# A reordered opening of the projection stage, key transposes without a staged copy, and an earlier load of the first remaining weight block

## What is computed

```python
h = rmsnorm(x, norm_pre);  p = in_proj(h, w_in)
# conv:  y = B * conv3(C * h_conv) * silu(z_conv), depthwise, causal, 256 channels
# nsa:   o = g0 * o_cmp + g1 * o_slc + g2 * o_win, g = sigmoid(gate), times silu(z)
x = x + rmsnorm(concat(nsa, gla, conv) @ w_out, norm_post)
```

## Time and profile before

| what | value |
|---|---|
| median of three executions | 1030.3 us |
| the profiled execution, its own time | 1031.92 us |
| its span | 1030.2 us |
| VectorE, ScalarE, GpSimd busy | 58%, 40%, 20% of the span |
| mean granted TensorE clock | 0.955 of full |
| most used DMA queue | 18.9% of 16 engines |

### The profile page before, as it was taken

The page is one execution under the profiler, slowest core; times in us unless marked ns, Lnnn a source line. Parts: engine busy times, 40 slices in busy tenths (PEclk is TensorE's granted clock), DMA queues, the critical chain, the costliest instruction groups (busy, mean ns, idle before and its releaser), DMA issues. The chain is left out here.

```text
span 1030.2 us, 16718 instructions
## 1 busy us (share of the span) xinstructions
PE 937.7 (91%) x5935; PEld 811.0 (79%) x5935; DVE 601.8 (58%) x1437; ACT 412.5 (40%) x918; POOL 201.7 (20%) x180
## 2 busy tenths in 40 slices
PE   2999999999969998999899978999788999999997
PEld 2999999999968987777789867777545676777765
DVE  3632010176434666778744567788648877787663
ACT  4533221111032545666534445666444434444322
POOL 3009599999320000000000050000000000000000
PEclk9999999999979999999999988999878999999999
DMA  6216634435051110000011012400334446453321
GB/s 208 93 53 198 245 103 142 162 112 165 1 180 43 52 42 28 9 1 1 1 43 50 23 46 68 138 1 1 140 112 115 117 135 187 135 150 103 117 88 32
DMA packets 106820, 93.73 MB, mean 91 GB/s; under 512 B 21245, under 2 KB 99954, under 8 KB 104626
## 3 DMA queue, kind: packets, MB, share of 16 engines
q1 hardware_dynamic: 84946, 58.65, 18.9%
q10 hardware_dynamic: 19488, 17.25, 5.5%
q0 software_dynamic: 2304, 16.78, 4.6%
HBM read 78.16 MB, written 18.61 MB: 94 GB/s over the span
## 5 line engine op out<-in xcount | busy, mean ns | idle before, releaser
L588 PE MATMUL ps<-w_hi,h_hi 128*128 128x264 f32 (+5 forms) x432 | 124.1, 287 | 0.5 <-DVE h_lo L457 0.5
L588 PE MATMUL ps<-w_hi,h_lo 128*128 128x264 f32 (+5 forms) x432 | 123.0, 285 | 0.0
L588 PE MATMUL ps<-w_lo,h_hi 128*128 128x264 f32 (+5 forms) x432 | 123.0, 285 | 0.0
L1276 DVE TENSOR_TENSOR pt_lo<-ps,pt_hi 128x512 fp32r<-128x512 f32 x132 | 90.9, 688 | 52.5 <-ACT pt_hi L1192 51.9
L1192 ACT ACTIVATE pt_hi<-ps 128x512 fp32r<-128x512 f32 x132 | 78.6, 597 | 83.5 <-PE ps L1099 82.7
L465 DVE TENSOR_TENSOR w_lo<-w_raw,w_hi 128x1024 fp32r<-128x1024 f32 (+2 forms) x12 | 29.1, 2426 | 122.4 <-ACT w_hi L366 122.4
L1272 DVE TENSOR_REDUCE least<-ps 128x1 f32<-128x640 f32 (+7 forms) x128 | 90.0, 703 | 14.0 <-PE ps L1088 12.7
L313 POOL TENSOR_TENSOR chunk<-chunk 128x1024 f32<-128x1024 f32 (+2 forms) x46 | 82.0, 1783 | 3.6
L588 PEld LDWEIGHTS ps<-w_hi,h_hi 128*128 128x128 f32 (+1 forms) x432 | 79.7, 185 | 1.3 <-issue 1.2
L588 PEld LDWEIGHTS ps<-w_lo,h_hi 128*128 128x128 f32 (+1 forms) x432 | 79.7, 184 | 0.0
L588 PEld LDWEIGHTS ps<-w_hi,h_lo 128*128 128x128 f32 (+1 forms) x432 | 79.4, 184 | 0.0
(11 more groups left out here) (382 smaller groups left out, 2285.5 us busy)
## 6 DMA issues: line engine op xcount, KB each, us to landing
kv_pages<-in_cache_slc_kv SPq DMA_DIRECT2D x256, 64.0 KB, 1.9
shared<-in_x_prompt SPq DMA_DIRECT2D x8, 512.0 KB, 3.6
w_raw<-in_w_in SPq DMA_DIRECT2D x8, 512.0 KB, 3.9
wr_raw<-in_w_in SPq DMA_DIRECT2D x8, 512.0 KB, 4.0
kv_window<-in_cache_win_kv SPq DMA_DIRECT2D x4, 1024.0 KB, 5.3
wo_raw<-in_w_out SPq DMA_DIRECT2D x8, 512.0 KB, 8.4
out<-in_cache_win_kv SPq DMA_DIRECT2D x1, 4032.0 KB
x_row<-in_x_prompt ACTq DMA_DIRECT2D x7, 512.0 KB, 5.1
```

What stands on the lines that cost most here:

```text
L588: mm = nc.tensor.matmul(out, lhs, rhs, start=(k == 0 and i == 0), stop=(k == KD - 1 and i == 2))
L1276: nc.vector.tensor_tensor(pt_lo[:, t % PTS, :], ps[:, turn_bank(t), :], pt_hi[:, t % PTS, :].bitcast(F32), ALU.subtract).then_inc(s_ptl, 1)
```

## The change

- VectorE starts with `normed(0)`; the page numbers come behind all tiles; the low halves of blocks 0 and 1 are VectorE's, after the scaled halves of tiles 0 and 1; `normed(t + 1)` stands between the two loops of `halves(t)`.
- The convolution's blocks are in the order c, h, z, b; a `b` take waits for the `z` take of the same columns.
- Rest block 0 is loaded in `project`, at the turn of block 8, into a place that the first stage does not use then (upper part of `w_raw`); three of its "w_split" steps stand ahead of the first "k_turn" and the fourth behind it.
- `k_st` and its copies are gone: TensorE transposes columns of `pk` with both key heads side by side, and ScalarE and VectorE read the 64 PSUM rows of their head.
- The gates' sigmoid is a tanh of ScalarE in `project` and one VectorE instruction (0.5 t + 0.5) at the start of `attend_prompt`.

```diff
...
+            at_w = -(-nc.sbuf_base // 32) * 32
+            w_next = nc.alloc_sbuf_tensor_at("wr_raw", [P, KD, P], F32, offset=at_w + 4 * KD * P)
...
-    CHAN = [("chbz"[m], h, c + h * P) for h in range(2) for m, c in enumerate((C_C, C_H, C_B, C_ZC))]
+    CHAN = [("chzb"[m], h, c + h * P) for h in range(2) for m, c in enumerate((C_C, C_H, C_ZC, C_B))]
...
+                    if b == NTB + 2:
+                        sp.dma_start(w_next[:, :, :], w_in[0, :, C_Z:C_Z + P].rearrange("(k p) c -> p k c", p=P)
+                                     ).then_inc(s_wr, 16)
...
-                for b in range(2):
-                    pool.wait_ge(s_whi, b + 1)
-                    nc.gpsimd.tensor_tensor(half(w_lo, b), raw(b), half(w_hi, b).bitcast(F32), ALU.subtract
-                                            ).then_inc(s_wlo, 1)
...
+                    if b == NTB:
+                        wait_taken(act, (NTB - 2, NT - 1))
+                        nc.scalar.activation(pk[:, 0:NT, K_GATE:NK], pk[:, 0:NT, K_GATE:NK], ACT.Tanh, scale=0.5)
...
                             ps[:, 6 + f, 0:4 * rows].rearrange("p (k c) -> p k c", k=4),
                             g_col[:, 4 * f:4 * f + 4].unsqueeze(2).to_broadcast([P, 4, rows]),
                             ALU.mult).then_inc(s_xg, 1)
+                    if t < 2:
+                        split(t)
+                    if t + 1 < T1:
+                        normed(t + 1)
                     for f in range(2):
                         dve.wait_ge(s_hi, 2 * t + f + 1)
                         nc.vector.tensor_tensor(
                                 src[:, n_p:tn].rearrange("p (b t) -> p b t", b=DB), ALU.mult)
                         ins.then_inc(s_td, 1)
                     elif what == "b":
+                        wait_taken(dve, (b - 1, c))
                         nc.vector.tensor_tensor(y_t[:, t0:t0 + tn], y_t[:, t0:t0 + tn], src, ALU.mult
                                                 ).then_inc(s_td, 1)
...
                         dve.wait_ge(s_tanh, n + 1)
                         did(nc.vector.scalar_tensor_tensor(tanh[:, n % 2, 0:tn], tanh[:, n % 2, 0:tn], 1.0, src,
                                                            ALU.add, ALU.mult))
-                        wait_taken(dve, (b - 1, c))
                         nc.vector.scalar_tensor_tensor(y_t[:, t0:t0 + tn], y_t[:, t0:t0 + tn], 0.5,
                                                        tanh[:, n % 2, 0:tn], ALU.mult, ALU.mult
                                                        ).then_inc(s_td, 1)
...
                 nc.vector.memset(eps[:, :], EPS).then_inc(s_ident, 1)
+                normed(0)
+                dve.wait_ge(s_g, 16)
+                for t in range(T1):
+                    halves(t)
                 dve.wait_ge(s_pg, 48)
                 dve.wait_ge(s_iota, 1)
                 did(nc.vector.tensor_scalar(page16[:, :], pages[:, :], float(NCH), None, ALU.mult))
                 nc.vector.tensor_tensor(rows16[:, :], chunk_no[:, :], page16[:, :].to_broadcast([P, NCH]),
                                         ALU.add).then_inc(s_idx, 1)
-                dve.wait_ge(s_g, 16)
-                normed(0)
-                normed(1)
-                for t in range(T1):
-                    halves(t)
-                    if t + 2 < T1:
-                        normed(t + 2)
                 split(2)
                 split(3)
                 dve.wait_ge(s_lo, 2 * T1)
...
-                    elif kind(b) == "z":
+                    elif kind(b) == "b":
                         v.wait()
                         wait_taken(dve, (b, 2))
                         nc.vector.memset(start[:, 0:1], 0.0).then_inc(s_conv, 1)
...
+                if kv == 0:
+                    for j in range(KD // 2 - 1):
+                        yield "w_split", 0, j
                 for b in range(4):
                     yield "k_turn", kv, b
-                    if b == 1 and kv == 0:
-                        for j in range(KD // 2):
-                            yield "w_split", 0, j
+                    if b == 0 and kv == 0:
+                        yield "w_split", 0, KD // 2 - 1
                     if b > 0 or kv > 0:
                         yield from fill(4)
...
-        w_raw = sb("wr_raw", [P, KD, P])
+        w_raw = w_next
         w_hi = sb("wr_hi", [P, KD, P], F32R)
+        sb("wr_raw_place", [P, KD, P])
         w_lo = sb("wr_lo", [P, KD, P], F32R)
...
-        k_st = prob[0][:, :, :].rearrange("p g n -> p (g n)")[:, 0:3 * NT * P].rearrange(
-            "p (n t a d) -> p n t a d", n=3, t=NT, a=2)
...
-        gate = sb("gate", [P, NT, 3 * NKV * NG])
+        gate = pk[:, 0:NT, K_GATE:NK]
...
-        s_wr, s_whi, s_wlo = sem("rest_w_loaded"), sem("rest_w_hi"), sem("rest_w_lo")
+        s_wr, s_whi, s_wlo = L.s_wr, sem("rest_w_hi"), sem("rest_w_lo")
...
-                load_w(0)
...
                     if what == "k_turn":
-                        if y == 0:
-                            pe.wait_ge(s_stg, x + 1)
                         if y >= 2:
...
                         for t in range(4):
-                            mm = nc.tensor.transpose(
-                                ps[:, 4 + 2 * (y % 2), t * P:(t + 1) * P],
-                                k_st[:, y // 2, 4 * (y % 2) + t, :, :].rearrange("p a d -> p (a d)"),
-                                ident[:, :])
+                            c = (K_SLC, K_WIN)[y // 2]
+                            mm = nc.tensor.transpose(ps[:, 4 + 2 * (y % 2), t * P:(t + 1) * P],
+                                                     pk[:, 4 * (y % 2) + t, c:c + NKV * HD], ident[:, :])
                         mm.then_inc(s_kt, 1)
...
                         for j in range(NT):
                             mm = nc.tensor.matmul(ps[:, 4, 2 * j:2 * j + 2],
-                                                  k_st[:, 2, j, :, :].rearrange("p a d -> p (a d)"), wk2[:, :],
+                                                  pk[:, j, K_CMP:K_CMP + NKV * HD], wk2[:, :],
                                                   start=True, stop=True)
...
-                nc.scalar.activation(gate[:, :, :], pk[:, 0:NT, K_GATE:NK], ACT.Sigmoid).then_inc(s_gate, 1)
-                nc.scalar.preload_act_table_set("exp_and_others")
...
                         b = y if what == "k_turn" else 4
                         act.wait_ge(s_kt, 6 * x + b + 1)
-                        dst = kT[:, b // 2, 512 * (b % 2):512 * (b % 2) + 512] if b < 4 else kcT[:, :]
-                        nc.scalar.activation(dst, ps[:, 4 + 2 * (b % 2), 0:512 if b < 4 else NB],
+                        dst = kT[0:HD, b // 2, 512 * (b % 2):512 * (b % 2) + 512] if b < 4 else kcT[0:HD, :]
+                        nc.scalar.activation(dst, ps[x * HD:(x + 1) * HD, 4 + 2 * (b % 2), 0:512 if b < 4 else NB],
...
+                nc.vector.tensor_scalar(gate, gate, 0.5, 0.5, ALU.mult, ALU.add).then_inc(s_gate, 1)
                 for what, x, y in steps:
                     if what == "k_stage":
-                        if x > 0:
-                            dve.wait_ge(s_pt, first_tile[PER_KV * x - 1])
-                        for a in range(2):
-                            for n, c in enumerate((K_SLC, K_WIN, K_CMP)):
-                                last = nc.vector.tensor_copy(k_st[:, n, :, a, :],
-                                                             pk[:, 0:NT, x * HD + c:x * HD + c + HD])
-                        last.then_inc(s_stg, 1)
                         if x == 0:
                             stage_query(0)
...
                     elif what in ("k_turn", "c_keys"):
                         b = y if what == "k_turn" else 4
                         dve.wait_ge(s_khi, 5 * x + b + 1)
-                        dst = kT[HD:P, b // 2, 512 * (b % 2):512 * (b % 2) + 512] if b < 4 else kcT[HD:P, :]
-                        nc.vector.tensor_tensor(dst, ps[HD:P, 4 + 2 * (b % 2), 0:512 if b < 4 else NB],
-                                                dst.bitcast(F32), ALU.subtract).then_inc(s_klo, 1)
+                        hi, lo = [kT[r, b // 2, 512 * (b % 2):512 * (b % 2) + 512] if b < 4 else kcT[r, :]
+                                  for r in (slice(0, HD), slice(HD, P))]
+                        nc.vector.tensor_tensor(lo, ps[x * HD:(x + 1) * HD, 4 + 2 * (b % 2), 0:512 if b < 4 else NB],
+                                                hi.bitcast(F32), ALU.subtract).then_inc(s_klo, 1)
```

More of the change, by code:

```diff
@@ L106, in hybrid_step @@
                 nc.sbuf_tensor("prob_win", [P, NG, WIN + P], F32) as prob_win:
-            project(nc, sem, ident, pq, pk, pn, kc, h_hi, h_lo, prob_win, s_cst, s_out, ps, va_dram, conv_dram,
+            at_w = -(-nc.sbuf_base // 32) * 32
+            w_next = nc.alloc_sbuf_tensor_at("wr_raw", [P, KD, P], F32, offset=at_w + 4 * KD * P)
+            project(nc, sem, ident, pq, pk, pn, kc, h_hi, h_lo, prob_win, s_cst, s_out, w_next, L.s_wr, ps, va_dram, conv_dram,
```

(8 more changed lines are left out.)

## The result

The changed kernel took 1013.93 us (median of five executions, 1013.81 to 1020.7); the kernel before, beside it, took 1028.99 us. The ratio is 0.9857, with a 95% interval of 0.9831 to 0.9882: 14.7 us (12 to 17) less, where 12.4 less and 1018 us had been forecast, in a range of 1010 to 1026. The profiled execution was the slowest of the five, 1020.7 us.

The account below looks back on a forecast made before the run. Time is won where TensorE, busy 937.7 of 1030.2 us, waits with nothing to do. Terms -7.7 + 2.8 - 6.0 - 1.5 + 0 gave -12.4 us, so 1018 us as a median, range 1010 to 1026.

Parts of the forecast that it names:

- The opening: Start of the first stage: block 0's product with tile 1 starts at 20.9 in place of 28.58, -7.7 us.
- The order: Block 10 in the first stage: z takes before the split delay its low half, stalling TensorE, +2.8 us.
- The multiply at 234.71 would meet the split: At block 10: beside GpSimd's 3.66 us multiply the split ends at 239.6, where TensorE needs it at 236.65.
- Rival 1: No stall at block 10, as GpSimd's phase has moved by 1.4 us and VectorE passes: 1013.6 us, chance 0.24.
- The border: Between first and second stage: keys turned at once, first rest product at 288.5 in place of 294.51, -6.0 us.
- The second key head: Before the second key head's transposes in the second stage: the wait for six key copies goes, -1.5 us.
- The clock: Granted clock behind waits: -1.5 us at the stage border, +1.5 behind block 10's stall, 0 together, bounds -4.5 and +3.5.
- The sum: All terms over the whole kernel: -7.7 + 2.8 - 6.0 - 1.5 + 0 = -12.4 us.
- Rival 3: First stage: x tiles arrive late and TensorE waits at seven tiles, so slower, 1037 us, chance 0.03.
- Rival 4: Rest block 0 is loaded during projections but split in the next stage; earlier splits give the same time; no chance given.

Follow-up runs that it names:

- the opening alone: Kernel before with only VectorE starting at tile 0, page numbers last and low halves of blocks 0 and 1 on VectorE: 1020.15 us, ratio 0.9914.
- border alone: Kernel before with only early load and splits of rest block 0, no key copies and gates by tanh: 1024.55 us, ratio 0.9944.
- the split ahead: Changed kernel with the split of block 10 ahead of the z takes on ScalarE and VectorE: 1007.45 us, and 1009.47 us once more.

## Why the prediction was right, step by step

- **The opening** (-7.7): measured -8.6 in the profile and 8.9 with the opening alone. Right. The 0.9 is gathered over VectorE's chain, which ends its last low halves of h at 19.84 and not at 20.7; the largest part, 0.5, are the low halves of h, 1.29 us for two where 1.47 was taken. The sum had left out that tile 2's transposes stand ahead of this product: from 19.3, with 1.94 us, they would have ended at 21.2. They took 1.09. The part that the text gave to page numbers against low halves was not priced separately; alone, the page numbers move the product by 2.1 us.
- **The order** (+2.8, bounds 0 and 5.6): the stall was 4.82 us, 4.8 to 4.9 in three profiles with this order and the gather in its place. Direction and mechanism were right, the size was not: the step that failed is "The multiply at 234.71 would meet the split". It met the third take, and the split then met an addition as well, 4.46 + 3.36 where the term had one meeting. The upper bound of 5.6 was this very case, with 4.47 and 3.92; it should have been the term. Taking the gain at the border off, this part costs more than it gives: undoing it gave 0.9778 against 0.9844.
- **Rival 1** (no stall, since GpSimd's phase has moved by 1.4 us): its time of 1014 was measured, but for another reason. The stall is there in the execution of 1013.67 us too, so that 1013.93 is nearer to this rival than to 1018 says nothing for it. Its premise was wrong twice: the page numbers end 0.3 us behind the tiles, and a first gather 13 us later left the phase at block 10 where it was.
- **The border** (-6.0): -6.5. Right. 0.9 us of it are the transposes at full clock, of which 0.5 was lost to the wait for the first low half. Without the early load and splits the border gives 1.8 us.
- **The second key head** (-1.5): its wait is gone. Right.
- **The clock** (0: -1.5 at the border, +1.5 behind the stall): it fell behind the stall as foreseen (5.7 us low), and cost 2.4 us in that piece and not 1.5. At the border it gave more than 1.5: 4.9 us low became 0.3 there, and 18.9 became 13.4 behind it, where the piece shrank by 4.2 with only 1.5 of it the second head's wait.
- **The sum**: from the first to the last piece but one the profiles differ by -14.2 us where -12.4 was forecast. The stall with its clock cost 6.6 and not 4.3; opening (-8.6), border with the stretch behind it (-10.7 in place of -9.0) and the last rest products (-1.5, no term) gave 4.1 more than forecast. So the total is close because misses of both signs cancel, which is luck in part. The last piece, where nothing was changed, then adds +3.0 in this pair of profiles. By the medians the miss is 2.3 to 2.7 us of 12.4.
- **Rival 3** (late tiles) did not show: no wait on the transposes beyond tile 2. **Rival 4**: the diff was what counted, as taken. Its "the same time" for earlier splits wasn't tried; the first rest product waited 0.50 us for a low half, so it needn't hold.

What stays open is the part of the clock in the sum of the parts. Opening and border alone give ratios of 0.9914 and 0.9944, together 0.986; the kernel with both and the old order has 0.9778, some 8 us less. The profiles put that into low clock: 92 us in the kernel before, 79 and 89 us with one part alone, 54 with both. Why fewer low stretches come when the two are joined isn't shown; a part may be chance, as the changed kernel alone went from 85 to 64 us between two profiles.

The best versions of the study that compute everything are the changed kernel with the split ahead (1007.45 and 1009.47 us, ratios 0.9772 and 0.9796) and the one with the old order (0.9778), which the measurements don't tell apart; the change itself has 0.9844 to 0.9857. The Trainium skill (SBUF — State Buffer, section "Who interferes with whom") says that a VectorE instruction with two SBUF inputs and a GpSimd instruction that reads SBUF shut each other out for a whole instruction; the 4.45 to 4.47 us beside 3.65, in all thirteen profiles that have the multiply, and 0.54 and 1.22 once GpSimd's sums are gone, agree with it.

## What to carry to other kernels

A reordering that puts more instructions ahead of a weight split has to be priced with more than one meeting with the neighbour engine: here a take met the multiply and the split behind it met the additions. Moving the split ahead of the takes cost nothing and won 5 to 9 us by the ratios. Two waits can cover each other, as the key copies and the load do here: with the copies alone gone the border gave 1.8 of 5.4 us (the early load alone wasn't tried). And a forecast finer than half a per cent needs to know how the granted clock varies between executions of one kernel: cutting two profiles at the same instructions shows which pieces differ, and how much low clock each has.

## What the runs showed of the hardware that I had not expected

- VectorE and GpSimd fall into step: in thirteen profiles GpSimd's multiply starts 0.64 or 0.65 us behind one VectorE instruction of the convolution and 0.39 or 0.40 us behind one of a z take. With the first gather 13 us later a multiply stands within 0.3 us of the same place at 225 us (the thirteenth in place of the fourteenth), and the stall is 4.28 in place of 4.82 us.
- One gather of 1 MB took 22.7 us from issue to landing where the median of sixteen was 5.7; 22.9 in the kernel before, 21.5 with the later gather. GpSimd stands still for some 10 to 12 us behind it.
- A small VectorE instruction can be long beside GpSimd: the index instruction on 32 columns took 1.30 us in the kernel before and 0.18 us in the changed one.
- The time at low clock in the same 2245 products of the last piece went from 39.9 to 61.0 us over the profiles, and the piece from 431 to 439 us, in kernels whose instructions there are the same; the shortest piece and the least low time go together, but 53.5 us came with 438.0 and 61.0 with 435.7.
